# A hybrid attention/retention/experts trunk: expert outputs through scratch memory, a wider in-projection, and rotation shared with VectorE

## The chip, the cores and the metric

One core of a Trainium2 chip runs the whole program. The metric is the time of one execution in microseconds, from the device; the kernel before took 1190.69 us (median of 3 runs, 1189.79 to 1190.95).

## What is computed

Two layers on 256 tokens of width 1024, in fp32. Each layer is a mixer and a channel mixer, both with a residual:

```python
h = rms_norm(x, ln_mix[l]);  proj = h @ w_in[l]                # 1024 x 2304
aq, ak, av, rq, rk, rv, rg = split(proj)                       # 512,128,128,256,256,512,512
ya = window_sink_attention(aq, ak, av, bias, sinks[l])
yr = gated_retention(rq, rk, rv, rg)                           # rq, rk are rotated by position
x  = x + concat(ya, yr) @ w_out[l]
h = rms_norm(x, ln_ffn[l])
x = x + (swiglu(h, ...) if l == 0 else moe_swiglu(h, ...))     # D_FF 2816; top 2 of 8 experts
return rms_norm(x, ln_final)
```

Layer 0 has a dense SwiGLU, layer 1 eight experts of that size; a token's result is the sum of its two experts' outputs by their gates.

## The kernel before

**Pieces.** All weights stream from memory once. SyncE loads units of 1 MB into a ring of 11 slots (L429 to L460 for the front, `load_expert` L462 for an expert) and waits, before it uses a slot again, until VectorE is done with what the slot held (`lo_vec`). A unit is two pieces of 128x1024. ScalarE rounds each piece to fp32r (`w_hi`, L372 and L392, 6 buffers), VectorE subtracts that from the raw piece (`w_lo`, L381 and L399, 3 buffers), and TensorE multiplies three times: high weights by high and low activations, then low weights by high activations (`piece`, L1164 to L1189; every matmul is recorded at L1144). Each engine's program is written out by hand piece by piece; at iteration s, ScalarE makes the high part of piece s+6 and VectorE the low part of s+3 after whatever else stands at s.

**Mixer.** 18 pieces of in-projection in nine column units of 256 (`IN_UNITS`; two pieces to a unit, 24 matmuls of 256 columns each), then 8 pieces of out-projection. After a unit's second piece ScalarE copies the sums of token tile t=0 out of PSUM into `proj` (L627) and VectorE those of t=1 (L863). The rest hangs on the iteration number s: at 6 the attention queries and keys are transposed, at 7 the scores (VectorE L880 to L885, ScalarE exp L640), at 9 the division of the probabilities (VectorE, eight `prob` L900), at 12 their transposition, at 13 the rotated retention queries and keys (`RET_TURN`). The rotation runs on GpSimd (`rope`, L508 to L529), at s=7 for the queries and at s=9 for the keys, four operations for each token tile.

**Start.** In layer 0 the position bias takes a way through memory: TensorE makes its rows after piece 0, ScalarE copies them out (L611), SyncE writes them (L434), waits, reads them back skewed (L441), loads the constants (L442), and then goes on with unit 5.

**Routing.** After layer 1's mixer: logits, top 2 and ranks on VectorE (L987 to L1021) while TensorE multiplies to no purpose between its few steps (`keep_busy`, L1373), slot masks `pick` (L1027), and then `gather` (L1397): the tokens of two experts are picked by matmuls of 256 columns with `xg_hi` and `xg_lo`, followed by four small ones with `rstd`. VectorE meanwhile makes `xg_lo` (L1061) and the gates (L1062 to L1071).

**One expert** (`act_expert` L736, `vec_expert` L1075, `tensor_expert` L1437): 44 pieces of gate and up, 22 of down, with 128 token slots. Its output stands in banks 6 and 7. At the start of the next expert ScalarE rounds it (`output_high` L730), VectorE makes the low part (`output_low` L1038), TensorE spreads the 128 slots over the 256 tokens by eight matmuls of 512 columns with `put` (`spread_out` L1419, after piece 3; `put` is `pick` transposed, two transposes at L1483), and VectorE adds the four tiles to `x_sb` by the gates (`add_output` L1045). After every second expert the next pair's tokens are gathered.

**End.** The last expert's output goes the same way; then squares, root and factor token tile by token tile, and three output DMAs on SyncE (L496, L500).

Of the kernel before, what the change touches and what calls it, by code (L numbers as in the profile page):

```python
# [9 lines left out]
I32 = mybir.dt.int32  # L10
ALU = mybir.AluOpType
# [3 lines left out]
P = 128  # L15
# [25 lines left out]
HIGHS, LOWS = 6, 3  # L41
IN_N = 256
IN_UNITS = D_IN // IN_N
# [24 lines left out]


WARM_COPY, WARM_CHOICE, WARM_MARK = 2, 8, 3  # L70
# [12 lines left out]
C_ALL = C_RANK + TT * N_EXPERTS  # L83
CHOSEN = 1000.0


def constants():
# [16 lines left out]
    for t in range(TT):  # L104
        rows = theta[t * P:(t + 1) * P].astype(np.float64)
        c[:, C_COS + 64 * t:C_COS + 64 * (t + 1)] = np.cos(rows)
        c[:, C_SIN + 64 * t:C_SIN + 64 * (t + 1)] = np.sin(rows) * sign
        c[:, C_RANK + 8 * t:C_RANK + 8 * (t + 1)] = np.arange(8, 0, -1)
    return c
# [31 lines left out]
def trunk(nc, x, ln_mix, w_in, w_out, rel_bias_table, sinks, ln_ffn, ffn_w_gate, ffn_w_up, ffn_w_down,  # L141
          router_w, exp_w_gate, exp_w_up, exp_w_down, ln_final, consts, buckets, out):
    with ExitStack() as ctx:
# [12 lines left out]
        ssum = sb("ssum", [P, 2])  # L156
        rvar = sb("rvar", [P, 8])
# [12 lines left out]
        gatex = sb("gatex", [P, TT, 16])  # L170
        rstd_e = sb("rstd_e", [P, 2])
# [37 lines left out]
        o_sq = at("o_sq", 18432, [P, TT, 512])  # L209
        probT = at("probT", 28672, [P, NCH, PAIRS * 128])  # L210
# [26 lines left out]
        oe_lo = at("oe_lo", 34816, [P, D_MODEL], F32R)  # L237

# [15 lines left out]
        def proj_bank(layer, u, t):  # L254
            return 4 + (2 * u + t + 2 * layer) % 4
# [24 lines left out]

        skew = nc.dram_tensor("skew", [ATT_HEADS, 64, REL], F32, kind="Internal").ap()
# [25 lines left out]
        att_done, ya_hi, ya_lo = sem("att_done"), sem("ya_hi"), sem("ya_lo")  # L307
        roped, r_turned, r_ready = sem("roped"), sem("r_turned"), sem("r_ready")
# [12 lines left out]
        pick_turned, put_ready = sem("pick_turned"), sem("put_ready")  # L321
        oe_hi_made, oe_lo_made, spread = sem("oe_hi_made"), sem("oe_lo_made"), sem("spread")
        rstd_gathered, rstd_e_made = sem("rstd_gathered"), sem("rstd_e_made")
        out_made0, out_made1, out_written = sem("out_made0"), sem("out_made1"), sem("out_written")
        vec_links, pool_links = sem("vec_links"), sem("pool_links")
# [80 lines left out]
        def _(sp):  # L406
# [22 lines left out]
            for u, (kind, layer, v) in enumerate(front):  # L429
# [16 lines left out]
                if u == 0:  # L446

                    for half in range(2):
                        dst = raw_piece(0, half).rearrange("p (k n) -> p k n", k=DK // 2)
                        src = w_in[0, half * 4 * P:(half + 1) * 4 * P, 0:IN_N]  # L450
                        sp.dma_start(dst, src.rearrange("(k p) n -> p k n", p=P)).then_inc(
                            raw_landed[0] if half else first_landed, 16)
                elif kind == "in":
                    dst = raw[:, slot, :].rearrange("p (k n) -> p k n", k=DK)
                    src = w_in[layer, :, v * IN_N:(v + 1) * IN_N]
# [39 lines left out]
            sp.wait_ge(out_made0, 1)  # L495
            sp.dma_start(out[0, 0:P, :], y[:, 0, :]).then_inc(out_written, 16)  # L496
# [8 lines left out]
        def _(pool):  # L505
            pool.dma_start(sink_all[:], sinks.rearrange("l h -> (l h)").partition_broadcast(P)).then_inc(sinks_landed, 16)

            def rope(layer, part):  # L508

                u = 3 + part  # L510
                pool.wait_ge(proj_act, IN_UNITS * layer + u + 1)
                pool.wait_ge(proj_vec, IN_UNITS * layer + u + 1)
                if part == 0:

                    pool.wait_ge(qk_turned, layer + 1)
                    pool.wait_ge(c_landed, 16)
                for t in range(TT):
                    src = proj[:, t, u * IN_N:(u + 1) * IN_N].rearrange("p (h d) -> p h d", d=64)
                    dst = proj[:, t, part * IN_N:(part + 1) * IN_N].rearrange("p (h d) -> p h d", d=64)
                    tmp = rope_tmp[:, t * IN_N:(t + 1) * IN_N].rearrange("p (h d) -> p h d", d=64)  # L520
# [11 lines left out]
            for layer in range(DEPTH):  # L532
                for s in range(MIX_PIECES):
# [8 lines left out]
                    if s == 7:  # L542
                        rope(layer, 0)
                    if s == 9:
                        rope(layer, 1)
# [973 lines left out]
```

## Time and profile before

| what | value |
|---|---|
| median of 3 runs | 1190.69 us |
| the profiled execution | 1190.02 us, its span 1188.0 us |
| TensorE busy | 1167.3 us, 98% of the span |
| VectorE, ScalarE busy | 975.7 us, 828.6 us |
| GpSimd busy | 30.9 us |
| moved by DMA | 344.64 MB, 290 GB/s over the span |

A busy TensorE is not TensorE at its peak, since matmuls are pipelined and their ends are modelled: what counts is how far apart their starts are. The front (both mixers and the dense layer) takes the first 386 us, routing up to 405, the experts up to 1175.

### The profile page before, as it was taken

What the parts mean: (1) busy time and instruction counts of PE and PEld (TensorE: products, weight loads), DVE (VectorE), ACT (ScalarE), POOL (GpSimd) and SP (SyncE); (2) the same over time, 40 slices, a digit from 0 to 9 for tenths busy, and PEclk for the clock granted to TensorE, in tenths of its full rate; (3) what the DMA queues carried; (4) which work ended last, traced back from release to release, by engine and by line L of the source; (5) the groups of instructions that cost most, each with busy time, mean ns of one, the idle gap of its engine ahead of it and who ended that gap; (6) DMA issues with size and microseconds to landing.
All of it is one profiled execution on the core that took longest, in us unless ns stands there. A gap on an engine that the chain in (4) does not pass through costs nothing.

```text
span 1188.0 us, 18370 instructions
## 1 busy us (share of the span) xinstructions
PE 1167.3 (98%) x6010; PEld 981.9 (83%) x6010; DVE 975.7 (82%) x1101; ACT 828.6 (70%) x1007; POOL 30.9 (3%) x43
## 2 busy tenths in 40 slices
PE   7999999999999999999999999999999999999996
PEld 7997888888998788888888888888888888888885
DVE  4867555545675999999899999989999989999996
ACT  6655554534653788878778778868887877887884
POOL 0400000000120000000000000000000000000000
PEclk9999999999999999999999999999999999999999
DMA  9955655556444399999899999989999999999960
GB/s 284 370 182 164 196 192 194 177 183 207 142 161 142 109 376 364 395 342 368 330 338 369 372 373 360 355 331 347 362 396 342 361 336 338 375 365 368 366 238 35
DMA packets 142614, 344.64 MB, mean 290 GB/s; under 512 B 6112, under 2 KB 64688, under 8 KB 142528
## 3 DMA queue, kind: packets, MB, share of 16 engines
q1 hardware_dynamic: 141952, 342.34, 80.3%
q0 software_dynamic: 352, 1.09, 0.4%
q8 instruction: 50, 0.82, 0.3%
q14 instruction: 36, 0.29, 0.1%
q10 hardware_dynamic: 224, 0.10, 0.1%
HBM read 342.06 MB, written 1.44 MB: 289 GB/s over the span
## 4 chain that ended last, share of the span: by engine, by line
PE 91%; DVE 4%; ACT 2%; DMA 2%; issue 1%; SPq 0%; DVEq 0%; ACTq 0%
PE psum L1144 87%; PE psum L1141 4%; DMA raw<-in_w_in 1%; DVE prob L900 1%; DVE w_lo L381 0%; DVE smax L884 0%; DVE score L880 0%; ACT w_hi L372 0%; DMA skew<-bias_rows 0%; DVE nmax L885 0%; ACT aT_hi L590 0%; DVE x_sb L828 0%; ACT squares L578 0%; ACT aT_hi L726 0%; ACT w_hi L392 0%
## 5 line engine op out<-in xcount | busy, mean ns | idle before, releaser
L399 DVE TENSOR_TENSOR w_lo<-raw,w_hi 128x1024 fp32r<-128x1024 f32 x528 | 627.3, 1220 | 40.9 <-PE psum L1144 15.7
L392 ACT ACTIVATE w_hi<-raw 128x1024 fp32r<-128x1024 f32 x528 | 550.2, 1061 | 110.1 <-PE psum L1144 108.3
L1144 PE MATMUL psum<-w_hi,aT_hi 128*128 128x512 f32 (+1 forms) x1232 | 447.2, 372 | 1.4 <-ACT w_hi L372 0.6
L1144 PE MATMUL psum<-w_hi,aT_lo 128*128 128x512 f32 (+1 forms) x1232 | 440.0, 366 | 0.0
L1144 PE MATMUL psum<-w_lo,aT_hi 128*128 128x512 f32 (+1 forms) x1232 | 323.3, 366 | 0.8 <-DVE w_lo L381 0.7
L1144 PEld LDWEIGHTS psum<-w_hi,aT_hi 128*128 128x128 f32 x1232 | 233.4, 189 | 38.6 <-issue 1.8
L1144 PEld LDWEIGHTS psum<-w_hi,aT_lo 128*128 128x128 f32 x1232 | 233.6, 190 | 35.0
L1144 PEld LDWEIGHTS psum<-w_lo,aT_hi 128*128 128x128 f32 x1232 | 214.6, 189 | 40.4 <-DVE w_lo L399 1.8
L381 DVE TENSOR_TENSOR w_lo<-raw,w_hi 128x1024 fp32r<-128x1024 f32 x118 | 144.8, 1234 | 48.7 <-PE psum L1144 44.6
L372 ACT ACTIVATE w_hi<-raw 128x1024 fp32r<-128x1024 f32 x118 | 124.6, 1059 | 82.4 <-PE psum L1144 74.2
L1144 PE MATMUL psum<-w_hi,heT_hi 128*128 128x512 f32 x352 | 138.1, 392 | 0.0
L1144 PE MATMUL psum<-w_hi,heT_lo 128*128 128x512 f32 x352 | 137.1, 389 | 0.0
L1144 PE MATMUL psum<-w_lo,heT_hi 128*128 128x512 f32 x352 | 108.5, 389 | 0.0
L1144 PEld LDWEIGHTS psum<-w_lo,heT_hi 128*128 128x128 f32 x352 | 66.1, 188 | 13.9
L1144 PEld LDWEIGHTS psum<-w_hi,heT_lo 128*128 128x128 f32 x352 | 66.1, 188 | 13.5
L1144 PEld LDWEIGHTS psum<-w_hi,heT_hi 128*128 128x128 f32 x352 | 66.1, 188 | 13.4
L760 ACT ACTIVATE heT_hi<-psum 128x512 fp32r<-128x512 f32 (+1 forms) x48 | 27.1, 564 | 26.4 <-PE psum L1141 26.4
L1100 DVE TENSOR_TENSOR heT_lo<-psum,heT_hi 128x512 fp32r<-128x512 f32 (+1 forms) x48 | 31.0, 646 | 6.1 <-ACT heT_hi L760 5.5
L755 ACT ACTIVATE hid_e<-psum,rstd_e 128x512 f32<-128x512 f32 (+1 forms) x48 | 29.6, 651 | 7.4 <-PE psum L1144 7.4
L1093 DVE SCALAR_TENSOR_TENSOR hid_e<-psum,rstd_e,hid_e 128x512 f32<-128x512 f32 (+1 forms) x48 | 32.4, 702 | 2.4 <-PE psum L1144 2.4
L1144 PE MATMUL psum<-w_hi,hdT_hi 128*128 128x512 f32 x88 | 34.3, 390 | 0.0
L1144 PE MATMUL psum<-w_hi,hdT_lo 128*128 128x512 f32 x88 | 34.3, 389 | 0.0
(179 smaller groups left out, 638.5 us busy)
## 6 DMA issues: line engine op xcount, KB each, us to landing
raw<-in_exp_w_down SPq DMA_DIRECT2D x88, 1024.0 KB, 7.1
raw<-in_exp_w_gate SPq DMA_DIRECT2D x80, 1024.0 KB, 7.0
raw<-in_exp_w_up SPq DMA_DIRECT2D x80, 1024.0 KB, 6.9
raw<-in_w_in SPq DMA_DIRECT2D x17, 1024.0 KB, 5.4
raw<-in_ffn_w_gate SPq DMA_DIRECT2D x22, 512.0 KB, 4.0
raw<-in_ffn_w_up SPq DMA_DIRECT2D x22, 512.0 KB, 5.1
raw<-in_ffn_w_down SPq DMA_DIRECT2D x11, 1024.0 KB, 5.0
raw<-in_w_out SPq DMA_DIRECT2D x8, 1024.0 KB, 8.1
```

The source lines that it names most:

```text
L372: nc.scalar.activation(high_slot(p), raw_piece((p // 2) % RING, p % 2), ACT.Copy).then_inc(hi_made, 1)
L381: eng.tensor_tensor(low_slot(p), raw_piece((p // 2) % RING, p % 2), high_slot(p).bitcast(F32), ALU.subtract).then_inc(lo_vec, 1)
L392: nc.scalar.activation(w_hi[:, q % HIGHS, :], raw_piece(slot, q % 2), ACT.Copy).then_inc(hi_made, 1)
L399: eng.tensor_tensor(w_lo[:, q % LOWS, :], raw_piece(e_slot[q // 2], q % 2), w_hi[:, q % HIGHS, :].bitcast(F32), ALU.subtract).then_inc(lo_ ...
L755: nc.scalar.activation(hid_e[:, c % 2, 0:E_CHUNKS[c][1]], gate_chunk(c), ACT.Silu, scale=rstd_e[:, j:j + 1]).then_inc(e_gate, 1)
L760: nc.scalar.activation(heT_hi[:, col // P:(col + width) // P, :], psum[:, 4 + c % 2, 0:width].rearrange("p (k t) -> p k t", t=P), ACT.Copy ...
L900: dve.tensor_tensor(prob[:, c, :, dst0:dst0 + 64], score[:, c, :, src0:src0 + 64], r, ALU.mult).then_inc(prob_ready, 1)
L1093: dve.scalar_tensor_tensor(out=part, in0=up_chunk(c), scalar=rstd_e[:, j:j + 1], in1=part, op0=ALU.mult, op1=ALU.mult).then_inc(e_hid, 1)
L1100: dve.tensor_tensor(heT_lo[:, cols, :], psum[:, 4 + c % 2, 0:width].rearrange("p (k t) -> p k t", t=P), heT_hi[:, cols, :].bitcast(F32), A ...
L1141: return pe.matmul(dst, src, ident, is_transpose=True, start=True, stop=True, skip_group_check=True)
L1144: return pe.matmul(dst, a, b, start=start, stop=stop, skip_group_check=True)
```

## The change

1. **Expert outputs through memory.** For the experts 0 to 6, `output_scaled` on ScalarE multiplies the output by the slot's gate into `oe` (the 4 KB a partition that `oe_lo` had), and GpSimd scatters its 128 rows by an indirect DMA into `scratch`, 1024 rows of 4 KB in memory: a token's first expert writes row n, its second row 256+n (rows from 512 on are for a second pass, which runs only if an expert has over 128 tokens). `spread_out`, `output_low`, `add_output` and the two transposes stay for expert 7 alone. `scratch` is cleared by two DMAs of 2 MB on GpSimd's queue in the middle of the dense layer. Within expert 7 GpSimd waits for all scatters and reads back four tiles of 128 rows, one after another into one buffer; VectorE adds them to `x_sb` at pieces 10, 18, 26, 34. Row numbers come from the routing: `info` holds rstd, gate and row of each token and expert, and `gather_info` and `slot_info` bring them to the slots after piece 1 and at piece 3 of every second expert (in place of the four `rstd` matmuls in `gather`).
2. **In-projection in blocks.** The columns go in blocks of 512, 256, 512, 512, 512. Pieces of a 512 block have 12 matmuls of 512 columns, the loads rows of 2 KB instead of 1 KB, and PSUM is copied out once a block (s = 3, 5, 9, 13, 17).
3. **Rotation.** GpSimd rotates token tile 0 only (queries and keys together, at s=9); VectorE rotates tile 1 out of PSUM at s=9 instead of copying it, by four operations.
4. **Start.** VectorE clears two tiles, and TensorE multiplies them 7 times before the first transposes and 3 times between them; `keep_busy` multiplies 10 and 5 times where it did 8 and 3.
5. **Routing.** ScalarE makes the high part of expert 0's first piece before the exponential, loads the table of Silu right behind it and makes pieces 1 and 2. TensorE gathers in the order high t=0, high t=1, low t=0, low t=1. VectorE makes the gathered low parts and `w_lo` of piece 0 ahead of the gates, then builds `info`.
6. **End.** Pieces 64 and 65 of expert 7 are multiplied half by half, the spread and the squares go half by half, both token tiles share one factor, and the output of tile 0 is issued by ScalarE.

```diff
@@ sizes
+IN_BLOCKS = [(0, 512), (512, 256), (768, 512), (1280, 512), (1792, 512)]
+NB = len(IN_BLOCKS)
+IN_UNIT_BLOCK = [0, 0, 1, 2, 2, 3, 3, 4, 4]
+IN_LAST = {3: 0, 5: 1, 9: 2, 13: 3, 17: 4}
+EARLY = 3
-WARM_COPY, WARM_CHOICE, WARM_MARK = 2, 8, 3
+WARM_COPY, WARM_CHOICE, WARM_MARK = 2, 10, 5
+START_BUSY = 7
+BACK = {10: 0, 18: 1, 26: 2, 34: 3}
@@ SyncE: loads of in_w_in
-                    src = w_in[layer, :, v * IN_N:(v + 1) * IN_N]
+                    src = w_in[layer, row:row + ks * P, col:col + width]
@@ GpSimd
+            def rope(layer):
+                pool.wait_ge(proj_act, NB * layer + 3)
+                pool.wait_ge(qk_turned, layer + 1)
+                pool.wait_ge(c_landed, 16)
+                src = proj[:, 0, COL_RQ:COL_RV].rearrange("p (h d) -> p h d", d=64)
...
+                if layer == 0:
+                    pool.wait_ge(piece_used, first + MIX_PIECES + GU_PIECES // 2)
+                    for r in range(2):
+                        pool.dma_start(scratch[r * ROWS:(r + 1) * ROWS, :], zeros).then_inc(scratch_cleared, 16)
...
+            def scatter_pass(r):
+                for e in range(LAST):
+                    v, j = e // 2, e % 2
+                    pool.wait_ge(rstd_e_made, N_PAIRS * r + v + 1)
+                    pool.wait_ge(oe_made, 2 * LAST * r + (2 * e + 2))
+                    pool.indirect_dma_start(scratch, bass.IndirectOffsetOnAxis(ap=row_e[:, v % 2, j:j + 1], axis=0), oe[:], None,
+                                            bounds_check=2 * ROWS - 1, oob_is_err=False).then_inc(scattered, 16)
+                pool.wait_ge(scattered, 16 * LAST * r + 16 * LAST)
+                for m in range(4):
+                    if m > 0:
+                        pool.wait_ge(back_added, 4 * r + m)
+                    pool.dma_start(back[:], rows[4 * r + m, :, :]).then_inc(back_landed, 16)
@@ ScalarE: after xg_hi; the outputs; the end
+            high_part_e(act, 0, 0)
             act.wait_ge(gap_made, 1)
             nc.scalar.activation(rc[4][:], rc[3][:], ACT.Exp).then_inc(e2_made, 1)
+            nc.scalar.activation(table_first[:], ssum[:, 0:1], ACT.Silu)
+            for q in range(1, EARLY):
+                high_part_e(act, 0, q)
...
+            def output_scaled(r, e):
...
+                    nc.scalar.activation(oe[:, 512 * b:512 * (b + 1)], bank(6 + b), ACT.Copy,
+                                         scale=info_e[:, v % 2, j, 1:2]).then_inc(oe_made, 1)
...
+            act.dma_start(out[0, 0:P, :], y[:, 0, :]).then_inc(out_written, 16)
@@ VectorE: start, block 2 of the in-projection
+            dve.memset(aT_lo[:, DK - 2:DK, :].bitcast(F32), 0.0).then_inc(zeros_made, 1)
...
+                        if col == COL_RQ:
...
+                            dve.scalar_tensor_tensor(out=dst, in0=src, scalar=rstd[:, 2, 1:2], in1=cos,
+                                                     op0=ALU.mult, op1=ALU.mult).then_inc(rope_links, 1)
+                            dve.scalar_tensor_tensor(out=tmp[:, :, 0::2], in0=src[:, :, 1::2], scalar=rstd[:, 2, 1:2], in1=sin[:, :, 0::2],
+                                                     op0=ALU.mult, op1=ALU.mult).then_inc(rope_links, 1)
+                            dve.scalar_tensor_tensor(out=tmp[:, :, 1::2], in0=src[:, :, 0::2], scalar=rstd[:, 2, 1:2], in1=sin[:, :, 1::2],
+                                                     op0=ALU.mult, op1=ALU.mult).then_inc(proj_vec, 1)
...
+                            dve.tensor_tensor(dst, dst, tmp, ALU.add).then_inc(roped_vec, 1)
@@ VectorE: routing, after xg_lo
+            for b in range(2):
+                gather_low(0, b)
+            low_part_e(dve, 0, 0)
             link.also(dve.tensor_scalar(posx[:, :, 8:16], posx[:, :, 0:8], -float(P), None, ALU.add))
...
-            for r in range(2):
-                link.also(dve.tensor_tensor(gatex[:, :, 8 * r:8 * r + 8], gates, tmp, ALU.add))
+            link.also(dve.tensor_tensor(info[:, :, :, 1], gates, tmp, ALU.add))
+            for t in range(TT):
+                step = link if t == TT - 1 else link.also
+                step(dve.tensor_scalar(rest[:, t, :], mask[:, t, :], cst[:, C_ROW + t:C_ROW + t + 1], None, ALU.mult))
+            link.also(dve.scalar_tensor_tensor(out=info[:, :, :, 2], in0=hot2, scalar=float(SEQ), in1=rest, op0=ALU.mult, op1=ALU.add))
+            link(dve.tensor_copy(info[:, :, :, 0], wide(rstd[:, 2, :])))
+            dve.tensor_copy(table_first[:], info[:, 0, 0, 0:1]).then_inc(info_ready, 1)
@@ VectorE: one expert
-                if e > 0:
-                    output_low(i - 1)
                 for q in range(FFN_PIECES):
-                    if e > 0 and q == 3:
-                        add_output(i - 1)
+                    if j == 0 and q == 3:
+                        slot_info(v, e // 2 % 2)
+                    if e == LAST and q in BACK:
+                        add_back(r, BACK[q])
@@ TensorE
+            pe.wait_ge(zeros_made, 1)
+            multiply_zeros(START_BUSY)
...
-                for part in range(2):
+                for part, t in ((0, 0), (0, 1), (1, 0), (1, 1)):
...
+            def gather_info(r, e):
+                pe.wait_ge(info_ready, r + 1)
...
+                    if e == N_EXPERTS - 1 and q == FFN_PIECES - 2:
+                        last_two(i)
+                        break
...
-                    if e > 0 and q == 3:
-                        spread_out(i - 1, v)
+                    if j == 0 and q == 1:
+                        gather_info(r, e)
...
-                    if q == PICK_TURN:
+                    if e == LAST and q == PICK_TURN:
```

## Rows read from the trace of the kernel before

**Rows 1.** The page: busy time by engine (share of the span, instructions).

```profile
PE 1167.3 (98%) x6010; PEld 981.9 (83%) x6010; DVE 975.7 (82%) x1101; ACT 828.6 (70%) x1007; POOL 30.9 (3%) x43
```

**Rows 2.** The chain (start us, us, what), same place two experts apart.

```profile
859.21 53.60 PE psum L1144 x236
...
1053.44 53.60 PE psum L1144 x236
```

**Rows 3.** Timeline of TensorE (start us, us): first spreading matmul, next piece.

```profile
503.26 0.39 PE L1144 MATMUL psum<-oe_hi,put 128*128 128x512 f32 x1
...
505.12 0.39 PE L1144 MATMUL psum<-w_hi,aT_hi 128*128 128x512 f32 x1
```

**Rows 4.** Windows (us; busy PE, PEld, DVE, ACT, POOL; PEclk, DMA share, GB/s).

```profile
12.00:15.00 3.00, 3.00 (x16) 3.00 (x16) 3.00 (x6) 3.00 (x6) 0.00 (x0) 1.00 1.10 348
45.00:48.00 3.00, 3.00 (x27) 3.00 (x27) 2.86 (x7) 3.00 (x13) 0.71 (x1) 1.00 1.03 408
1025.00:1050.00 25.00, 25.00 (x118) 20.68 (x117) 23.44 (x23) 20.49 (x23) 0.00 (x0) 1.00 0.99 365
```

**Rows 5.** Waits of SyncE's queue, 430 to 1150 us (total us, times, longest).

```profile
SPq L473 <- DVE w_lo L399: 328.5, 140, 7.4
```

**Rows 6.** DMA issues (count, KB each, median us to landing).

```profile
raw<-in_exp_w_down SPq DMA_DIRECT2D x88, 1024.0 KB, 7.1
...
gain<-in_ln_ffn POOLq DMA_DIRECT2D x1, 512.0 KB, 5.8
```

**Rows 7.** Timeline of TensorE and ScalarE at the start.

```profile
14.74 1.70 PE L1144 MATMUL psum<-w_lo,aT_hi 128*128 128x256 f32 x8
...
33.50 1.06 ACT L372 ACTIVATE w_hi<-raw 128x1024 fp32r<-128x1024 f32 x1 [3.83 <-DMA raw<-in_w_in]
```

**Rows 8.** The chain: layer 0's transposes at s=6, layer 1's in-projection.

```profile
35.49 1.53 PE psum L1141 x12
...
296.43 20.38 PE psum L1144 x168
```

**Rows 9.** Timeline of VectorE and GpSimd around s=9 of layer 0.

```profile
40.66 0.42 DVE L880 SCALAR_TENSOR_TENSOR score<-psum,bias 128x256 f32<-128x256 f32 x1 [0.17 <-PE psum L1144]
...
49.64 0.47 DVE L863 TENSOR_SCALAR proj<-psum,rstd 128x256 f32<-128x256 f32 x1
...
50.52 5.07 DVE L900 TENSOR_TENSOR prob<-score,rden 128x256 f32<-128x256 f32 x8
55.51 3.00 DVE L381 TENSOR_TENSOR w_lo<-raw,w_hi 128x1024 fp32r<-128x1024 f32 x2
...
55.94 1.49 POOL L525 TENSOR_TENSOR rope_tmp<-proj,cst 128x128 f32<-128x128 f32 x1
```

**Rows 10.** Waits of TensorE, 35 to 110 us (total us, times, longest).

```profile
PE psum L1144 <- DVE w_lo L381: 0.4, 1, 0.4
```

**Rows 11.** Timeline of TensorE and VectorE in the routing.

```profile
398.35 3.65 PE L1144 MATMUL psum<-pick,xg_hi 128*128 128x256 f32 x16 [0.61 <-DVE pick L1027]
401.84 2.09 PE L1144 MATMUL psum<-pick,xg_lo 128*128 128x256 f32 x16
403.76 0.95 PE L1144 MATMUL psum<-rstd,pick 128*128 128x1 f32 x8
...
401.62 0.26 DVE L1071 TENSOR_TENSOR gatex<-rt,rt 128x16 f32<-128x16 f32 x2
403.28 1.29 DVE L1031 TENSOR_TENSOR aT_lo<-psum,aT_hi 128x512 fp32r<-128x512 f32 x2 [1.40 <-ACT aT_hi L726]
404.48 1.21 DVE L399 TENSOR_TENSOR w_lo<-raw,w_hi 128x1024 fp32r<-128x1024 f32 x1
```

**Rows 12.** A window of the routing (columns as rows 4).

```profile
400.00:402.00 2.00, 2.00 (x12) 2.00 (x12) 1.74 (x9) 1.99 (x4) 0.00 (x0) 0.56 0.02 4
```

**Rows 13.** Timeline of VectorE at the end: the additions, the last outputs.

```profile
1177.60 2.73 DVE L1051 SCALAR_TENSOR_TENSOR x_sb<-psum,gatex,x_sb 128x512 f32<-128x512 f32 x4 [0.39 <-PE psum L1144]
...
1183.46 1.41 DVE L1134 SCALAR_TENSOR_TENSOR y<-x_sb,rstd,cst 128x512 f32<-128x512 f32 x2
```

More of the change, by code:

```diff
@@ L141, in trunk @@
 def trunk(nc, x, ln_mix, w_in, w_out, rel_bias_table, sinks, ln_ffn, ffn_w_gate, ffn_w_up, ffn_w_down,
-          router_w, exp_w_gate, exp_w_up, exp_w_down, ln_final, consts, buckets, out):
+          router_w, exp_w_gate, exp_w_up, exp_w_down, ln_final, consts, buckets, zeros, out):
     with ExitStack() as ctx:
@@ L738, in act_expert @@
                 i, v, j = N_EXPERTS * r + e, N_PAIRS * r + e // 2, e % 2
-                for q in range(HIGHS):
-                    if e == 0 and q == 2:
+                for q in range(EARLY if e == 0 else 0, HIGHS):
+                    if e == 0 and q == EARLY:
                         for b in range(4):
@@ L1144, in mm, with multiply_zeros @@
                 return pe.matmul(dst, a, b, start=start, stop=stop, skip_group_check=True)
+            def multiply_zeros(count):
+                for again in range(count):
+                    mm(bank(4), aT_lo[:, DK - 1, 0:P], aT_lo[:, DK - 2:DK, :].rearrange("p k t -> p (k t)"), True, True)
             def turn_h(n):
@@ L1436, in _, with last_two @@
             n_pass = pe.value_load(passes_i[0:1, 0:1], min_val=1, max_val=2)
+            def last_two(i):
+                base = FFN_PIECES * i + FRONT_PIECES
+                for half in range(2):
+                    cols = slice(512 * half, 512 * (half + 1))
+                    for q in (FFN_PIECES - 2, FFN_PIECES - 1):
+                        if half == 0:
+                            pe.wait_ge(hi_made, base + (q + 1))
+                        mm(bank(6 + half), heT_hi[:, q - GU_PIECES, :], w_hi[:, q % HIGHS, cols], False, False)
+                        mm(bank(6 + half), heT_lo[:, q - GU_PIECES, :], w_hi[:, q % HIGHS, cols], False, False)
+                    for q in (FFN_PIECES - 2, FFN_PIECES - 1):
+                        if half == 0:
+                            pe.wait_ge(lo_vec, base + (q + 1))
+                        ins = mm(bank(6 + half), heT_hi[:, q - GU_PIECES, :], w_lo[:, q % LOWS, cols], False, q == FFN_PIECES - 1)
+                        if half == 1:
+                            ins.then_inc(piece_used, 1)
+                        elif q == FFN_PIECES - 1:
+                            ins.then_inc(down_half, 1)
             def tensor_expert(r, e):
```

319 lines of the change are left out of this document (189 added, 130 removed).

## The prediction

> **What bounds the kernel now.** The page comes first: TensorE is busy for 98% of the span, VectorE for 82%, GpSimd for 3% [rows 1]. Since a busy TensorE can be a slow one, I looked next for the distance between its matmuls, in the chain of waits. In the experts it is almost all TensorE: 236 matmuls of 512 columns take 53.60 us, 0.227 us each, with no gap, and the same place comes back after 1053.44 - 859.21 = 194.23 us, two experts [rows 2]. So the experts go at TensorE's pace, and each matmul taken out there is a gain. Two things stand close behind: DMA, share 0.99 at 365 GB/s, VectorE busy 23.44 of 25 us [rows 4]. But SyncE waited 328.5 us in 140 waits at L473 alone, 2.3 us each, for a slot to become free [rows 5], and a unit lands 7.1 us after issue [rows 6] where the ring reaches 10 units of 2.9 us ahead (194.23 us for 66): the stream is ahead of its use. Elsewhere the chain leaves TensorE at four places, all of which the change touches: the start, s=7 to 12 of each mixer, the routing, the end.
>
> **Experts 0 to 6, spreading removed.** Eight matmuls took 503.26 to 505.12 = 1.86 us [rows 3]; the two transposes of `pick` I take at 0.11 each, close to the small matmuls that stand 0.95 / 8 = 0.12 us apart [rows 11]. 2.08 us x 7 = 14.6 us, all of it on the path. VectorE loses two `oe_lo` and four additions of 0.68 us [rows 13], over 4 us an expert, so it doesn't become the bound; ScalarE's two copies stay. What must carry the new pace: a pair goes from 194.2 to 190.1 us, with 2 x 34.6 MB of weights (3 x 1024 x 2816 x 4 bytes) and 1 MB of scatters, 370 GB/s. Rows of 4 KB (the `w_out` loads) ran at 408 GB/s, rows of 1 KB at 348 [rows 4]; 27 of an expert's 33 units have rows of 4 KB. That is some 5% in hand, so nothing is charged. The scatters have an expert's time, about 90 us, before `oe` is written again. **-14.6 us.**
>
> **Reading back in expert 7.** Four additions of 128x1024, 1.2 us each at the price of a `w_lo` [rows 11], take the place of those removed. The price can lie in the round trips: addition, issue on GpSimd, landing. A direct load of 512 KB on that queue landed after 5.8 us [rows 6], others of 1 MB after 7.1. First come the copies of expert 6, the scatter (no row shows an indirect DMA; nearest are the 5.8 and 7.1 us) and the first load: about 1 + 7 + 7 + issue = 16 to 18 us, while VectorE reaches the first addition after ten pieces of 6 x 0.227 = 1.36 us, 14 us, and has some 3 us before TensorE misses the next low part. Later steps have 8 pieces, 10.9 us, for about 9. Between 0 and 6 us; I take **+1.0**, near the lower end, since the landing rows fit the steps.
>
> [...]
>
> **Clearing.** Two DMAs of 2 MB in the dense layer, where the ring is full and half the DMA time is free: the cover is the ring's 10 units. 0; without cover, at 408 GB/s for 8 MB, 20 us would be the end.
>
> **In-projection, blocks.** 168 matmuls of 256 columns took 20.38 us, 0.1213 each (a few small ones among them make it about 0.120) [rows 8]; twelve of 512 for twenty-four of 256 make 2.73 for 2.88 us, -0.15 us for each of the 16 wide pieces of a layer.
>
> **Rotation.** In each mixer VectorE is without a pause from the first score (40.66 us) to the end of `w_lo` of piece 12, the first of the two from 55.51 (57.1), 16.4 us [rows 9], and TensorE waits 0.4 us for that part [rows 10]. There the copy of 0.47 us [rows 9] goes, and four operations come: by 0.68 us for 512 columns from PSUM [rows 13] about 0.7 + 2 x 0.4 + 0.6, with links 2.25 us; +1.8. GpSimd no longer works beside the scores, which gives back 0 to 1.5; I take 0.7, since it held up a `w_lo` by 0.3 [rows 9] and had eight operations there. After s=9 GpSimd has as many elements as before, so the eight `prob`, 5.07 us or 0.63 each [rows 9], stay slow. VectorE's stretch grows to 17.5 us, TensorE's shrinks by 0.7, and it stalls 2.2 us instead of 0.4. Layer 1: 6 wide pieces before (-0.9), +1.1, then 5.3 pieces (-0.8): -0.6 us. If the rotation costs nothing, a layer gains 2.4; if it meets GpSimd's port at every step, it loses 1.5.
>
> **Start and layer 0.** The first piece ran at half speed: 8 matmuls in 1.70 us, 0.21 apart [rows 7], where they later are 0.12 apart [rows 8]. With TensorE kept busy from 1.5 us on, I expect 2.73 instead of 5.1 us for that piece. But this gain, and that of pieces 1 to 6, ends at s=6: ScalarE can't copy block 1 before it has made the high part of piece 10, for which it waited 3.83 us for unit 5, landed at 33.5 us [rows 7], and the transposes came at 35.49 [rows 8]. Unit 5 comes earlier only as the loads do: rows of 2 KB lie between 348 and 408 GB/s; at 385 by the same cost for each row, with the bias's way through memory as before, I put it 1.15 us earlier (0 to 2.5). Then +1.1 and -0.9 as in layer 1. Layer 0: **-1.0**, both layers **-1.6 us**.
>
> **Routing.** TensorE picks the tokens from 398.35 us; the 16 `xg_hi` take 3.65 us, the 16 `xg_lo` 2.09 [rows 11], because the granted clock was 0.56 around [rows 12], nearly all of that window at 1.2 instead of 2.4 GHz, after a wait of 0.61 us [rows 11] and small matmuls. The added `keep_busy` fill such waits; at full clock the picks end at 402.2, bank 0 and 1 follow by ScalarE and VectorE (1.29 us for two, rows 11), and piece 0 starts at 403.6 instead of the 404.8 that follow the four small matmuls. It then needs `w_lo`, 1.21 us [rows 11], until 404.9. Now the new order bites. Before, eight small operations (the last ended at 401.9 [rows 11]) and the loading of `n_pass` ran while TensorE picked. Now they stand behind `w_lo` of piece 0, and there are twelve: at 0.1 without and 0.2 with a link, 1.9 us, then the load and the loop's entry, 1.6 us by the time from the last small one to the next VectorE operation (401.6 to 403.28 [rows 11]). `w_lo` of piece 1 is ready at 409.5; TensorE wants it at 406.3, and has `gather_info`, 0.95 us [rows 11], still to do. Piece 1 ends, that included, at 410.9 instead of 404.8 + 2.9 = 407.7: **+3.2 us**. If VectorE's queue hides the load, 1.5; if the gap of 3 us brings the clock down as before the picks, 1.5 us more; if the clock doesn't hold in the picks either, 6.
>
> **End.** Half 0 of the output is complete six matmuls, 1.37 us, earlier; rounding, low parts and spreading overlap, and the last addition ends at about 1179.3 for 1180.3 [rows 13]. The last square is half as wide (-0.5), and one factor serves both tiles, so VectorE isn't held by the first. y ends at 1183.2 for 1184.87 (1.41 us from 1183.46 [rows 13]): **-1.65** (-1 to -2).
>
> **Sum:** -14.6 + 1.0 - 1.6 + 3.2 - 1.65 = -13.65 us. The profiled execution took 1190.02 us, which makes 1176.4; the median stands 0.67 us higher, so 1177.0.
>
> **Rivals.** (a) The small places are hidden: VectorE's queue hides the routing's chain, GpSimd's absence frees the `prob`. Routing +0.5, mixers -4, reading back 0: 1170.9. For it: each of these is an estimate of order. Against: VectorE's stretch shows no pause. (b) TensorE's clock falls in the new gaps (2.2 us twice, 3.2 in the routing) and the rotation meets GpSimd: +1.5 for each clock, +1.5 a layer: 1184.5. For: 0.56 after smaller waits [rows 12]. Against: the gap I expect stands between pieces at full rate, not among small matmuls. (c) Slower: **DMA becomes the bound of the experts.** The stream reached a share of 0.99 at 365 GB/s [rows 4]; if writes to memory and scattered rows among the reads hold it at 355, a pair takes 70.2 MB / 355 = 197.8 us, 3.6 more than now, 14.3 more over four pairs, in place of a gain of 14.6; with the rest 1206. It decides from 370 GB/s down, and turns slower below about 363. Against: 408 GB/s, and 2.3 us of waiting at each slot. (d) The shared port holds up GpSimd's issues in expert 7: a first landing at 25 us instead of 17 costs 8 us, and three later trips of 13 us with their 1.2 us of addition, against steps of 10.9, cost 10: about 1194. It decides where a trip takes over 9.7 us. (e) The multiplied zeros don't raise the clock: the sum moves by under 1 us, because unit 5 holds the place.
>
> **Chances.** The forecast 0.50 (1173.5 to 1180.5), (a) 0.18, (b) 0.20, (c) 0.05, (d) 0.04, the rest elsewhere. The range reaches over (a) and (b): 1169.5 to 1185. No change is told from a measurement within about 0.2% (2.4 us). Faster 0.91, same 0.03, slower 0.06.
>
> **What would show it.** Right: 190.1 us for a pair, no `put` matmul outside expert 7; `xg_hi` at 0.12 us each with a clock of 1; TensorE waiting about 3 us for `w_lo` after piece 0, and about 2 us for it at s=12 of each layer; the s=6 transposes near 34.3 us. Wrong: pairs longer than 191 us with TensorE waiting for `w_hi` on a DMA; waits of VectorE for `back` of over 3 us; no stall at s=12.

## The result, and the profile after

The kernel after takes **1184.22 us** (median of 4 runs, 1182.96 to 1184.97) against 1190.57 us for the kernel before beside it: a ratio of 0.9946 [0.9929, 0.9964], a gain of 6.4 us where 13.65 were forecast. The profiled execution took 1184.97 us, its span 1183.2 (before: 1190.02 and 1188.0).

I cut the span at places that both kernels have: the transposes at s=6, each mixer's last transposes of x, the first down matmul of each expert, the last instruction.

| stretch | before | after | change | forecast |
|---|---|---|---|---|
| start to the s=6 transposes | 35.49 | 33.85 | -1.64 | -1.15 |
| rest of layer 0's mixer | 70.09 | 72.93 | +2.84 | +0.15 |
| dense layer | 188.27 | 188.33 | +0.06 | 0 |
| layer 1's mixer | 92.81 | 95.04 | +2.23 | -0.6 |
| routing, to expert 0's down | 80.97 | 86.56 | +5.59 | +3.2 |
| down of expert 0 to down of expert 6 | 582.71 | 569.06 | -13.65 | -12.5 |
| down of 6 to down of 7 | 94.57 | 95.25 | +0.68 | -1.1 |
| from there to the end | 43.06 | 42.13 | -0.93 | -1.65 |
| sum | 1187.97 | 1183.15 | -4.82 | -13.65 |

So the experts paid a little more than was forecast, and the front gave over half of it back. The page after, beside [rows 1]:

```profile
PE 1155.3 (98%) x5570; PEld 952.2 (80%) x5570; DVE 959.5 (81%) x1069; ACT 827.1 (70%) x995; POOL 28.0 (2%) x33
```

98% again. The share of busy time doesn't tell the two kernels apart; the distance between the starts of matmuls does. The chain in the experts, same place two experts apart, as in [rows 2]:

```profile
669.50 51.73 PE psum L1264 x228
...
859.18 51.73 PE psum L1264 x228
```

189.68 us for a pair instead of 194.23, 228 matmuls at 0.227 us. Then TensorE's waits in three windows: layer 0's mixer (35 to 110 us), the routing (404 to 420), expert 7 (1046 to 1142); total us, times, longest:

```profile
PE psum L1264 <- DVE w_lo L414: 2.8, 1, 2.8
...
PE psum L1264 <- DVE w_lo L432: 2.8, 1, 2.8
...
PE psum L1264 <- DVE w_lo L432: 1.7, 2, 1.3
```

The first stands against 0.4 in [rows 10], and layer 1 has the same 2.8. What follows the waits is in the windows (us; busy PE, PEld, DVE, ACT, POOL; PEclk, DMA share, GB/s):

```profile
57.30:60.70 3.40, 3.40 (x13) 2.92 (x13) 2.02 (x2) 0.60 (x1) 0.00 (x0) 0.50 1.10 347
340.60:344.00 3.40, 3.40 (x13) 2.91 (x13) 2.01 (x2) 0.60 (x1) 0.00 (x0) 0.50 0.43 92
412.20:419.00 6.80, 6.27 (x19) 5.30 (x20) 5.75 (x7) 1.80 (x2) 0.00 (x0) 0.50 0.75 257
```

In each, from the end of a wait on (in the routing from half a microsecond before it), TensorE's granted clock is 0.50, the lower level of 1.2 GHz, for 3.4, 3.4 and 6.8 us. PE is "busy" all through them: this loss shows in no list of waits. It shows in TensorE's timeline of the routing (the rows between are other matmuls of the same pieces):

```profile
401.84 2.14 PE L1264 MATMUL psum<-pick,xg_hi 128*128 128x256 f32 x16
...
407.38 0.49 PE L1264 MATMUL psum<-w_hi,aT_hi 128*128 128x512 f32 x1 [1.49 <-ACT aT_hi L787]
...
412.73 1.22 PE L1264 MATMUL psum<-w_lo,aT_hi 128*128 128x512 f32 x2 [2.78 <-DVE w_lo L432]
413.75 1.70 PE L1264 MATMUL psum<-info,pick 128*128 128x3 f32 x8
415.31 0.77 PE L1264 MATMUL psum<-w_hi,aT_hi 128*128 128x512 f32 x1
415.88 0.63 PE L1264 MATMUL psum<-w_hi,aT_lo 128*128 128x512 f32 x1
```

The picks run at full clock (2.14 us for 16, 3.65 in [rows 11]) and piece 0 starts 5.54 us behind the first of them, 6.46 before. From 412.73 us until the clock is back at 419 the matmuls of 512 columns stand 0.43 us apart instead of 0.23.

The other view is VectorE's and GpSimd's timeline around s=9 of layer 0, beside [rows 9]:

```profile
47.20 0.75 DVE L960 SCALAR_TENSOR_TENSOR proj<-psum,rstd,cst 128x512 f32<-128x512 f32 x1
47.86 0.48 DVE L962 SCALAR_TENSOR_TENSOR rope_vec<-psum,rstd,cst 128x256 f32<-128x256 f32 x1
...
48.84 0.69 DVE L968 TENSOR_TENSOR proj<-proj,rope_vec 128x512 f32<-128x512 f32 x1
49.45 1.28 DVE L1000 TENSOR_TENSOR psums<-psums,esink 128x16 f32<-128x16 f32 x1
...
51.05 4.87 DVE L1007 TENSOR_TENSOR prob<-score,rden 128x256 f32<-128x256 f32 x8
55.83 3.48 DVE L414 TENSOR_TENSOR w_lo<-raw,w_hi 128x1024 fp32r<-128x1024 f32 x3
...
49.22 1.47 POOL L553 TENSOR_TENSOR proj<-proj,cst 128x512 f32<-128x512 f32 x1 [27.32 <-ACT proj L684]
50.65 0.86 POOL L554 TENSOR_TENSOR rope_tmp<-proj,cst 128x256 f32<-128x256 f32 x1
51.48 1.04 POOL L555 TENSOR_TENSOR rope_tmp<-proj,cst 128x256 f32<-128x256 f32 x1
52.59 1.36 POOL L557 TENSOR_TENSOR proj<-proj,rope_tmp 128x512 f32<-128x512 f32 x1
```

`psums` adds the sinks to the sums of the exponentials, 16 elements a partition. It takes 1.28 us and ends at 50.73, when GpSimd's first operation (49.22 to 50.69) ends. In the kernel before GpSimd began its rotation of the keys only at 51.21, and the same operation read:

```profile
50.03 0.16 DVE L893 TENSOR_TENSOR psums<-psums,esink 128x16 f32<-128x16 f32 x1
```

The eight `prob` are done at 55.92; TensorE waits from 54.3 for the `w_lo` behind them.

### The profile page after: what moved, and what is told of

Its sections match the earlier page's. It is cut to its first block, busy times and chain, and to the rows that moved or that the text cites. A ratio compares the mean times of both kernels' runs of the same rounds, so it can differ in the third digit from the quotient of the medians.

```text
span 1183.2 us, 17331 instructions
## 1 busy us (share of the span) xinstructions
PE 1155.3 (98%) x5570; PEld 952.2 (80%) x5570; DVE 959.5 (81%) x1069; ACT 827.1 (70%) x995; POOL 28.0 (2%) x33
## 4 chain that ended last, share of the span: by engine, by line
PE 89%; DVE 4%; DMA 3%; ACT 2%; issue 1%; SPq 0%; DVEq 0%; ACTq 0%; POOLq 0%
PE psum L1264 85%; PE psum L1261 3%; DMA raw<-in_w_in 1%; DVE prob L1007 1%; DMA scratch<-oe,row_e 1%; DVE w_lo L432 1%; DMA back<-scratch 1%; DVE w_lo L414 0%; ACT w_hi L405 0%; DMA skew<-bias_rows 0%; DVE proj L1040 0%; ACT L728 0%; DVE psums L1000 0%; ACT proj L728 0%; ACT aT_hi L714 0%
## 5 line engine op out<-in xcount | busy, mean ns | idle before, releaser
L1264 PE MATMUL psum<-w_hi,aT_hi 128*128 128x512 f32 (+1 forms) x1104 | 433.8, 394 | 3.7 <-ACT w_hi L405 1.5
L1264 PE MATMUL psum<-w_hi,aT_lo 128*128 128x512 f32 (+1 forms) x1104 | 426.8, 388 | 0.0
L1264 PEld LDWEIGHTS psum<-w_lo,aT_hi 128*128 128x128 f32 x1104 | 206.0, 189 | 55.5 <-DVE w_lo L414 6.4
L1264 PEld LDWEIGHTS psum<-w_hi,aT_hi 128*128 128x128 f32 x1104 | 208.1, 188 | 46.1 <-issue 3.7
L1264 PEld LDWEIGHTS psum<-w_hi,aT_lo 128*128 128x128 f32 x1104 | 208.1, 189 | 39.9
L829 ACT ACTIVATE hid_e<-psum,info_e 128x512 f32<-128x512 f32 (+1 forms) x48 | 29.5, 651 | 7.3 <-PE psum L1264 7.3
L1211 DVE SCALAR_TENSOR_TENSOR hid_e<-psum,info_e,hid_e 128x512 f32<-128x512 f32 (+1 forms) x48 | 32.4, 704 | 2.2 <-PE psum L1264 2.2
```

The costliest lines, as they stand in the source:

```text
L829: nc.scalar.activation(hid_e[:, c % 2, 0:E_CHUNKS[c][1]], gate_chunk(c), ACT.Silu, scale=info_e[:, e // 2 % 2, j, 0:1]).then_inc(e_gate, 1)
L1211: dve.scalar_tensor_tensor(out=part, in0=up_chunk(c), scalar=info_e[:, e // 2 % 2, j, 0:1], in1=part, op0=ALU.mult, op1=ALU.mult).then_inc ...
L1264: return pe.matmul(dst, a, b, start=start, stop=stop, skip_group_check=True)
```

## The experiments

The theory from these views: most of the missing gain lies in the front: in three waits of TensorE, in the low clock behind each, and in VectorE and GpSimd stopping each other. The rivals: the rotation costs VectorE too much by itself, the scatters and the reading back hurt the experts, the zeros do nothing. All ratios are to the kernel before, run beside; stretches and waits are those of one profiled execution a kernel.

**rot_late: VectorE's rotation behind the probabilities.** The four operations move from s=9 to s=10, behind the eight `prob` and `w_lo` of piece 12.

```diff
-                        if col == COL_RQ:
...
-                            dve.wait_ge(c_landed, 16)
...
+                    if s == 10:
+                        u = 2
+                        dve.wait_ge(piece_used, first + 10)
...
+                        dve.wait_ge(c_landed, 16)
...
```

> The changed kernel with VectorE's rotation of token tile 1 moved from ahead of the probabilities (s=9) to behind them and behind w_lo of piece 12 (s=10). Theory 1: in each mixer TensorE's stall of 2.9 us at piece 12 comes from the four rotation operations (2.3 us) and the psums addition that runs into GpSimd's 1.47 us operation right behind them, and the half clock of 3.4 us that follows the stall costs another 1.7 us. Then the stall goes to under 0.5 us, there is no stretch at half clock at s=12, the second mixer (first transposes to first transposes behind it) goes from 95.0 us to about 90.5, and the time falls by 8 to 9 us, to about 1175.5. Rival: the blocks of 512 columns themselves (copies once per block, later) hold the mixers up: then the second mixer stays over 94 us and the time within 2 us of 1184.

Measured: 1179.58 us, 0.9914 [0.9898, 0.9931]. Layer 1's mixer came down from 95.04 to 92.37 us, not to 90.5: a wait of 1.4 us stays, because the eight `prob` (start us, us) grew to 6.33 us; GpSimd's four operations ran from 332.24 to 336.98 beside them.

```profile
331.26 6.33 DVE L1009 TENSOR_TENSOR prob<-score,rden 128x256 f32<-128x256 f32 x8
337.52 1.21 DVE L414 TENSOR_TENSOR w_lo<-raw,w_hi 128x1024 fp32r<-128x1024 f32 x1
```

Moving the work off the path is right, but 1.5 us of it (4.87 to 6.33) came straight back as slower `prob`. Behind this wait of 1.4 us the clock stayed at 1.00 in both layers. Layer 0's mixer came down by 1.0 us only, to 71.90: in this profile unit 5 landed later, TensorE waited 2.3 us ahead of the transposes at s=6 (34.60 us), and the clock was at 0.50 for 3.4 us behind that wait.

**rope_pool: GpSimd rotates both tiles again**, in the wide blocks; VectorE copies.

```diff
+                pool.wait_ge(proj_vec, NB * layer + 3)
...
+                for t in range(TT):
+                    src = proj[:, t, COL_RQ:COL_RV].rearrange("p (h d) -> p h d", d=64)
...
-                        if col == COL_RQ:
...
-                        else:
+                        if True:
...
```

> The changed kernel with both token tiles rotated by GpSimd at s=9 (eight operations) and VectorE only copying its 512 columns. Theory 1: VectorE's stretch loses about 1.6 us, but GpSimd works some 10 us beside the probabilities, so they stay slow; the stall at piece 12 falls from 2.9 to 1 to 2 us and the second mixer from 95.0 to 92 to 94 us; time 1178 to 1182. If it is no better than 1184, what VectorE saves is lost at the port it shares with GpSimd. Rival (blocks): no change, 1184.

Measured: 1187.33 us (10 runs, 1184.05 to 1191.48), 0.9978 [0.9963, 0.9992], 3.1 us more than the kernel after (whose interval ends at 0.9964, so the two just touch) and far from the 1178 to 1182 expected. Layer 1's mixer took 95.47 us, the wait at piece 12 was 3.2 us, and `prob`:

```profile
333.27 7.39 DVE L990 TENSOR_TENSOR prob<-score,rden 128x256 f32<-128x256 f32 x8
```

What VectorE saved in the rotation it lost in `prob`. So it isn't VectorE's share of the rotation that hurts, but when GpSimd has its own.

**pool_after: GpSimd begins when the probabilities are made.** One wait is added in `rope`.

```diff
                 pool.wait_ge(proj_act, NB * layer + 3)
+                pool.wait_ge(prob_ready, 8 * (layer + 1))
                 pool.wait_ge(qk_turned, layer + 1)
```

> The changed kernel with one wait more: GpSimd begins its rotation of token tile 0 only when VectorE's eight probability operations are done. Theory 1 (lock): in the changed kernel a psums addition of 0.17 us took 1.28 us and the eight prob took 4.87 us because each waits for a whole GpSimd operation at the shared port. Without it psums takes 0.17 us and the eight prob 2.6 to 3.0 us; the stall at piece 12 goes from 2.9 to under 0.3 us although the rotation on VectorE stays where it was, no half clock at s=12, second mixer 95.0 -> about 90.5, time 1175 to 1176. Rival 2 (VectorE's own rate): broadcast operands make prob slow by themselves, then they stay over 4.5 us and the stall over 2.3 us.

Measured: 1178.43 us, 0.9903 [0.9888, 0.9918]. VectorE's and GpSimd's timeline, same place:

```profile
49.62 0.17 DVE L1001 TENSOR_TENSOR psums<-psums,esink 128x16 f32<-128x16 f32 x1
...
50.11 2.77 DVE L1008 TENSOR_TENSOR prob<-score,rden 128x256 f32<-128x256 f32 x8
52.80 3.49 DVE L414 TENSOR_TENSOR w_lo<-raw,w_hi 128x1024 fp32r<-128x1024 f32 x3
...
53.02 4.41 POOL L554 TENSOR_TENSOR proj<-proj,cst 128x512 f32<-128x512 f32 x1 [31.36 <-DVE prob L1008]
57.39 0.87 POOL L555 TENSOR_TENSOR rope_tmp<-proj,cst 128x256 f32<-128x256 f32 x1
```

Of TensorE's waits there (total us, times, longest) this one is new:

```profile
PE psum L1262 <- POOL proj L558: 1.5, 1, 1.5
```

`psums` is back at 0.17 us, `prob` at 0.35 each instead of 0.61, the wait at piece 12 and the low clock behind it are gone in both layers. Now GpSimd is the one that is held up: its first operation, 1.47 us before, takes 4.41 and ends 1.1 us behind VectorE's three `w_lo` (56.3), whose own time didn't grow (3.49 us, 3.48 in the kernel after). The turn of the retention tiles waits 1.5 us for the last of its operations. That is why layer 1's mixer stops at 92.08 us, 1.6 above the 90.5 expected; layer 0's took 70.03.

The Trainium skill says of this pair of engines ("SBUF — State Buffer", section "SBUF: two separate sides") that their shared ports are a lock that whichever starts first holds for its whole instruction, and that a VectorE operation with two SBUF inputs takes part in it against a GpSimd operation that reads SBUF. The traces agree in both directions: the 16 elements of `psums` end with GpSimd's operation, 1.28 us instead of 0.17, and GpSimd's 4.41 us stand beside `w_lo`. They show one thing more: GpSimd was kept out for three `w_lo` in a row, not for one.

**before_pool_after: the same wait in the kernel before**, for its rotation of the keys.

```diff
+                else:
+                    pool.wait_ge(prob_ready, 8 * (layer + 1))
```

> The kernel before, with GpSimd's rotation of the retention keys held until VectorE's eight prob are made. If the two engines hold each other up, this was so before the change too: the eight prob of a layer take about 2.8 us instead of 5.07, and TensorE's 0.4 us wait at piece 12 goes. GpSimd's four operations for each tile then run beside w_lo and end about 3 us later, so the turn of the retention tiles may wait 1 to 2 us for them. Time: between 1188.5 and 1191.5 us, that is within about 1 us of the kernel before's 1190.4. Rival (prob is slow for a reason of its own, such as the broadcast of rden): prob stays at 5 us and the time is the same or 1 us longer.

Measured: 1189.92 us (10 runs: nine from 1188.86 to 1190.94, one of 2375.96 whose cause is open) against 1189.81, 1.0 [0.999, 1.001].

```profile
50.18 2.77 DVE L902 TENSOR_TENSOR prob<-score,rden 128x256 f32<-128x256 f32 x8
```

`prob` went from 5.07 to 2.77 us and the wait of 0.4 us at piece 12 went with it; the turn of the retention tiles did not wait for GpSimd. The mixers gained 0.3 us each. The lock cost the kernel before 2.3 us of VectorE in each layer and almost nothing in time, since there it was hidden. This run shows something else: its picks ran at full clock (2.15 us instead of 3.65) without the longer `keep_busy`, and piece 0 still came 6.54 us behind the first pick, 6.46 before, waiting for ScalarE's `aT_hi`.

**no_dip: TensorE multiplies on while it waits**, eleven useless matmuls in each of the three waits. Their results aren't used.

```diff
+                if busy:
+                    busy()
                 if i is None:
                     pe.wait_ge(lo_vec, p + 1)
...
+                            for again in range(11):
...
```

> The changed kernel with eleven matmuls of no use (2.5 us) in the wait of TensorE for w_lo of piece 12 of each mixer and of piece 1 of expert 0: the waits stay, the idle time goes. Theory 1: the half clock behind each wait is caused by the idle time, so it goes; the waits end where they ended; each mixer is 1.5 to 1.7 us shorter (second mixer 95.0 -> 93.4) and the routing stage 3 us (86.55 -> 83.5); time about 1178. Rival: the clock falls for another reason (small matmuls before), the dips stay and the time is 1184 or more.

Measured: 1179.57 us, 0.9913 [0.9898, 0.9928]. The windows over the three places (columns as above):

```profile
55.00:65.00 10.00, 9.73 (x56) 8.02 (x55) 8.74 (x12) 4.02 (x6) 0.00 (x0) 1.00 1.08 338
335.00:345.00 10.00, 9.73 (x55) 8.05 (x54) 8.84 (x13) 2.79 (x5) 0.67 (x1) 1.00 0.32 107
405.00:420.00 15.00, 14.73 (x69) 12.00 (x68) 13.40 (x27) 9.80 (x11) 0.00 (x0) 1.00 0.63 222
```

Clock 1.00 in each; `prob` still 4.87 us and the low parts no earlier. The stretches lost 1.57 us (layer 0 from s=6), 1.68 (layer 1) and 3.0 (routing). This is the price of the clock alone: 6.2 us in the profiled executions. The medians of the two kernels lie 4.7 us apart, and both kernels' executions spread over some 2 us.

**info_first: the routing's small chain ahead of the low parts.** `info` is made while TensorE picks, and `w_lo` of pieces 0 to 2 ahead of the loading of `n_pass`.

```diff
-            for b in range(2):
-                gather_low(0, b)
-            low_part_e(dve, 0, 0)
...
+            for b in range(2):
+                gather_low(0, b)
+            for q in range(LOWS):
+                low_part_e(dve, 0, q)
...
```

> The changed kernel with the gates and info made before the gathered low parts, and w_lo of pieces 0, 1 and 2 all ahead of the loading of n_pass. Theory 1: the wait of 2.9 us for w_lo of piece 1 and the 6.8 us at half clock behind it are both the order's doing; both go, piece 0 starts at most 0.3 us later, and from the first transposes behind mixer 1 to the steady place in expert 0 the stage falls from 89.7 us to about 84.5; time about 1179. Rival 1: the clock falls anyway, from the 1.65 us wait before piece 0: only the wait goes, -3 us. Rival 2: VectorE can't finish the chain before the gathered tiles are ready, and the wait moves ahead of piece 0: -1 us.

Measured: 1180.59 us, 0.9926 [0.9909, 0.9942]; routing 80.71 us instead of 86.56. The profiled execution took 1178.39 us, the shortest of four; the others took 1180.58 to 1181.29, so that the medians fell by 3.6 us only, and no profile shows where the rest went. VectorE's timeline:

```profile
405.62 0.15 DVE L1191 COPY smax<-info 128x1 f32<-128x1 f32 x1
405.69 1.28 DVE L1138 TENSOR_TENSOR aT_lo<-psum,aT_hi 128x512 fp32r<-128x512 f32 x2
406.89 4.62 DVE L432 TENSOR_TENSOR w_lo<-raw,w_hi 128x1024 fp32r<-128x1024 f32 x4
```

The chain ends at 405.77, 0.2 us behind ScalarE's first `aT_hi` (405.55), so it costs next to nothing here: piece 0 starts 5.71 us behind the first pick instead of 5.54. In the kernel after VectorE stood idle in that very place, 1.62 us before its `aT_lo`. The wait of 2.8 us and the low clock behind it go together.

**back_late: the reading back eight pieces later.**

```diff
-BACK = {10: 0, 18: 1, 26: 2, 34: 3}
+BACK = {18: 0, 26: 1, 34: 2, 42: 3}
```

> The changed kernel with the four additions of the read-back tiles at pieces 18, 26, 34, 42 of expert 7 instead of 10, 18, 26, 34. Theory 1: the first scatter and load take 16 us from the issue, longer than ten pieces; given eight pieces more, TensorE's waits in expert 7 (1.5, 0.5 and 0.2 us) go and the time falls by 2 to 2.5 us, to about 1182. Rival: expert 7 is short of VectorE time because of the additions themselves (4.9 us), then the waits move to other pieces and the time changes by under 0.7 us.

Measured: 1183.58 us, 0.9943 [0.9926, 0.996], with the intervals of the two kernels overlapping; the stretch from down 6 to down 7 went from 95.25 to 92.93 us, and VectorE no longer waits for `back`. Part of the gain was lost in layer 0's mixer, where the clock stayed low for 6.8 us instead of 3.4 in this profile. In the kernel after the chain of that expert reads:

```profile
1078.33 8.04 DMA scratch<-oe,row_e
1086.37 0.29 issue
1086.66 6.95 DMA back<-scratch
1093.63 0.05 DVE x_sb L1158
```

**no_scatter: no indirect DMA.**

```diff
-                    pool.indirect_dma_start(scratch, bass.IndirectOffsetOnAxis(ap=row_e[:, v % 2, j:j + 1], axis=0), oe[:], None,
-                                            bounds_check=2 * ROWS - 1, oob_is_err=False).then_inc(scattered, 16)
-                pool.wait_ge(scattered, 16 * LAST * r + 16 * LAST)
...
```

> The kernel after, without the seven indirect DMAs and the waits for them; the outputs of experts 0 to 6 are left out of the result, and expert 7 reads back zeros. If the scattered rows cost the weight stream and the engines nothing, two experts stay 189.7 us apart and the time stays within 0.5 us of 1184.2, except in expert 7, where the first read no longer waits behind a scatter of 8 us: VectorE's wait of 2.58 us for the first tile goes, expert 7 comes down from 95.25 to about 93 us, and the time is about 1182. Rival (the writes are paid for by the weights, or GpSimd's issue holds VectorE up): a pair falls below 189 us, and the time by 3 us or more below 1182.

Measured: 1183.34 us (1181.74 to 1186.88), 0.995 [0.9934, 0.9967]. Two experts stay 189.69 us apart, so the scatters take nothing from the weight stream. Down 6 to down 7 falls to 92.97, as expected; the median fell by 0.9 us only, within the spread of the executions.

**no_zeros: without the zeros at the start.**

```diff
...
-                        multiply_zeros(3)
...
-            pe.wait_ge(zeros_made, 1)
-            multiply_zeros(START_BUSY)
```

> The changed kernel without the matmuls on zeros at the start and between the first transposes. Theory 1: the first piece runs at half clock again (0.43 us for a matmul of 512 columns), but the transposes at s=6 still wait for ScalarE, held by the landing of unit 5, so they come within 0.3 us of 33.85 and the time stays at 1184. Rival: the zeros are what brought the transposes from 35.49 to 33.85; then they come at 35.0 or later and the time is 1.3 us longer.

Measured: 1185.37 us, 0.9959 [0.9943, 0.9975]. The first piece ran at half speed again (its matmuls of 512 columns stood 0.43 us apart, 0.23 in the kernel after; the clock's record begins only behind it), and the s=6 transposes came at 34.47 us instead of 33.85, between the expectation and its rival. But nine profiles with the zeros in have them anywhere from 33.85 to 34.60 (rot_late), and in no_dip, where the clock was at 0.50 from 11.2 to 14.6 us, they came at 33.92. So the zeros speed up the first piece, and no effect on the transposes or on the time stands out of the spread.

**mended: rot_late, pool_after, info_first and back_late together.**

> The changed kernel with four moves together: VectorE's rotation behind the probabilities, GpSimd's too, the gates and info ahead of the gathered low parts with w_lo of pieces 0 to 2 ahead of the loading of n_pass, and the read-back additions eight pieces later. Theory 1: the four costs add: two mixers 2 x 4.5, routing 5.8, expert 7 2.3: 1184.2 - 17.1 = about 1167, and the sum first predicted for the change without its new stalls. Rival: something else holds the mixers once the stall is gone (w_lo of piece 13 behind the late rotation, or the late rotation of tile 0 at the turning of the retention tiles), then a mixer gains 2 us at most and the time is about 1172.

Measured: **1168.83 us** (5 runs, 1168.57 to 1170.38), 0.9822 [0.9809, 0.9835]: 21.6 us under the kernel before, 15 under the kernel after. From s=6 layer 0's mixer took 68.85 us, layer 1's 90.88, the routing 80.67, down 6 to down 7 92.97. That is 1.8 us above the 1167 expected: the mixers gained 4.1 and 4.2 us where 4.5 each was added up. The only low clock left is at the very end, behind TensorE's last matmul. Its GpSimd and VectorE still stop each other, but where it costs TensorE no more than a wait of 0.3 us for `probT` in each mixer:

```profile
48.22 2.77 DVE L1010 TENSOR_TENSOR prob<-score,rden 128x256 f32<-128x256 f32 x8
...
54.58 4.10 DVE L414 TENSOR_TENSOR w_lo<-raw,w_hi 128x1024 fp32r<-128x1024 f32 x2
...
51.13 2.15 POOL L554 TENSOR_TENSOR proj<-proj,cst 128x512 f32<-128x512 f32 x1 [29.50 <-DVE prob L1010]
```

## Why the prediction was right or wrong

**The step that failed.** The sum had TensorE waiting at the right three places and for about the right time, but put the low clock behind these waits at 0. The reason given was that they stand between pieces at full rate. In all three the clock fell to 0.50, and by no_dip this cost 1.57 + 1.68 + 3.0 = 6.2 us of the 8.8 us between the forecast span and the measured one. The rest is mostly in the mixers and in the reading back.

**Experts: right.** 2.08 us was forecast for each; the spacings fell by 2.15 and 2.39 (94.57 to 92.42, 99.66 to 97.27). DMA held 189.7 us a pair, and no_scatter shows that the scatters were no part of the question. Rival (c) is out.

**Reading back: the trip right, its effect too small.** The first tile was forecast 16 to 18 us after expert 6's copies and came after 17.3 (1076.3 to 1093.6). What failed is the 3 us of slack given to VectorE: TensorE waited 1.7 us in all, and the stretch is 2.3 us above the same one in back_late. With +2.83 against 92.42, the same stretch one pair earlier, +1.0 should have been +2.8, of which back_late gives 2.3 back. Rival (d) did not decide: VectorE waited for one tile (2.58 us), not four, and GpSimd's four issues took 0.53 to 0.57 us each and landed within 4.8 to 7.3 us.

**Mixers: the stall too short, the clock left out.** The stall at s=12 was forecast at 2.2 us and is 2.8, both layers. Two terms were missing. First, "GpSimd no longer works beside the scores, which gives back 0.7" counted GpSimd's absence at s=7, but not that its operations now begin exactly at `psums` and hold that one up by 1.1 us; that "the eight `prob` stay slow" was right (4.87 for 5.07), and pool_after shows why they are slow and that they needn't be. Second, the clock: the forecast put it into rival (b) and the sum at 0. It cost 1.57 and 1.68 us by no_dip. -1.6 us for both layers became -1.64 + 2.84 + 2.23 = +3.4; some 3.3 of the difference of 5.0 are the clock; the lock and the longer stall are in the rest, which no run splits up.

**Routing: the wait right, the clock behind it not.** `w_lo` of piece 1 was forecast 11.15 us behind the first pick, and TensorE went on with it after 10.89; the wait of 3.2 us is 2.8. "If the gap brings the clock down, 1.5 us more" was the side case and came true, with twice the price: 3.0 us, since the low level lasted 6.8 us and lay over `gather_info` and two pieces. My argument against, that a gap between pieces at full rate would not bring it down, is refuted at all three places. And the faster picks, from which I took part of 1.2 us, were worth nothing by themselves: in before_pool_after they were fast and piece 0 came no earlier. Nor is the longer `keep_busy` shown to be what made them fast, since before_pool_after has the old one (the ten profiles with the new one all had full clock there). What brought piece 0 forward by 0.9 us, the new order of the picks, ScalarE's early pieces or the small matmuls that are gone, no run separates.

**Start: about right.** -1.64 for -1.15 up to s=6, where nine profiles with this start spread over 0.75 us. As said in (e), the faster first piece is not what counts: the transposes wait for ScalarE and that for unit 5. How much the wider rows and how much the blocks brought, no run separates.

**End: the computing right, the landing missed.** VectorE's last `y` ends 1.68 us earlier behind the same down matmul (39.96 to 38.28), as forecast. But the end is now 0.93 us earlier only: before, the last instruction's end came 3.1 us behind the last `y` (1184.87 to 1187.97), now 3.9 (1179.30 to 1183.15), with the first tile's 512 KB issued 0.2 us ahead of that end (1179.12, on ScalarE's queue) where it was 1.3 us ahead before (1183.53, on SyncE's). What lands last is in both kernels SyncE's second half of the other tile: before 2.7 us after its issue at 1184.90, now 3.4 us after its issue at 1179.32. ScalarE's tile is in 0.6 us before it. That the closer issues slow each other's landing was not tried.

**In sum** rival (b), 1184.5, described the outcome: clock at each new gap, rotation against GpSimd's port. The measured 1184.22 us is inside the range of 1169.5 to 1185 only because that range was drawn to reach over (b). That it lies within 0.3 us of (b) is partly luck: (b) had 1.5 us for the routing's clock where 3.0 were paid, and the experts' larger gain made up for part of the reading back and the end.

## What to carry to other kernels

Charge a new wait of TensorE with the low clock behind it: here 2.8 us of waiting cost 1.6 us more in a mixer and 3.0 in the routing, and eleven useless matmuls, or better the removal of the wait, gave it back. When work is split between VectorE and GpSimd, let GpSimd's part begin behind the VectorE operations that somebody waits for: one wait for a semaphore was worth 5.8 us here. And where an engine's chain is moved behind other work, look first for an idle place ahead of it; VectorE's idle time before `aT_lo` took in the whole chain of `info`.

## What was unexpected of the hardware

- A 16-element operation took 1.28 us instead of 0.17, and GpSimd's 1.47 us became 4.41, when they met the other engine's; which one paid depended on who had begun.
- The low clock came behind waits of 2.8 us amid pieces at full rate, for 3.4 or 6.8 us, not the same from one profile to the next (layer 0: 3.4 in the kernel after, 6.8 in back_late and rope_pool; routing: 6.8, but 3.4 in pool_after). Behind rot_late's 2.3 us in layer 0 it came too; behind rot_late's 1.4 us at s=12 and pool_after's 1.5 us it stayed at 1.00.
- An indirect DMA of 128 rows of 4 KB held GpSimd for 1.3 us and landed 8.0 us after its issue (median of 7), beside a full weight stream, against 6.9 to 7.3 us for the stream's own units of 1 MB; a pair of experts is as long with it as without.
